# Six weight splits of the recurrence stage, each moved to a later place in VectorE's program

## The reference

```python
z = rmsnorm(h, norm1_g[l])
proj = z @ w_in[l]
q, fl, iv, og, pin, ga, gb = jnp.split(proj, SPLITS, axis=-1)
o_a = hgrn2_mixer(q, fl + b_f[l], iv, og, lb_all[l], head_norm_g[l])   # 8 heads, S_t = diag(f_t) S_{t-1} + (1 - f_t) i_t^T
o_b = pool_mixer(pin, w_pool[l], pool_scale[l])                        # 4 groups: trailing mean minus the frame, a 128 x 128 product each
mix = jax.nn.sigmoid(ga) * (o_a @ w_branch_a[l]) + jax.nn.sigmoid(gb) * (o_b @ w_branch_b[l])
```

## Time and profile before

| | |
|---|---|
| profiled execution | 1472.77 us |
| its span | 1470.9 us |
| median of three runs | 1473.01 us |
| TensorE busy | 1450.9 us (99%) |
| VectorE busy | 834.5 us (57%) |
| ScalarE busy | 691.8 us (47%) |
| granted TensorE clock | 1.000 |

### The profile page before, as it was taken

One profiled execution on the slowest core, in us unless ns is written; L12 is line 12 of the kernel. 1 busy time (PEld: TensorE's weight loads), 2 busy tenths in 40 slices (PEclk: granted clock), 3 DMA queues, 4 the chain that ended last, 5 costly groups with the idle time before them and its releaser, 6 DMA issues.

```text
span 1470.9 us, 26479 instructions
## 1 busy us (share of the span) xinstructions
PE 1450.9 (99%) x11311; PEld 1283.2 (87%) x11311; DVE 834.5 (57%) x1365; ACT 691.8 (47%) x1025; POOL 115.7 (8%) x278
## 2 busy tenths in 40 slices
PE   7999999999999999999999999999999999999998
PEld 7999999999999898998888777788899888778888
DVE  6487977764656566654335787642223566644343
ACT  6565877853443222322233676542222777743232
POOL 0000000000000000000000044300000233320000
PEclk9999999999999999999999999999999999999999
DMA  7222121124322223222334333433223333342222
GB/s 245 87 75 80 60 87 59 59 73 143 131 88 87 86 90 112 87 86 85 103 101 108 63 48 20 77 97 105 86 86 90 67 71 71 72 106 92 86 94 80
DMA packets 138969, 130.25 MB, mean 89 GB/s; under 512 B 26569, under 2 KB 134884, under 8 KB 138596
## 3 DMA queue, kind: packets, MB, share of 16 engines
q1 hardware_dynamic: 134084, 120.39, 26.0%
q0 software_dynamic: 4752, 8.16, 5.3%
q10 hardware_dynamic: 16, 0.00, 0.0%
HBM read 119.69 MB, written 4.26 MB: 84 GB/s over the span
## 4 chain that ended last, share of the span: by engine, by line
PE 91%; DVE 4%; ACT 3%; issue 1%; DMA 0%; SPq 0%; DVEq 0%; ACTq 0%
PE PS L922 79%; PE PS L1248 3%; PE PS L1221 2%; PE PS L1204 2%; DVE wlo L1897 1%; PE PS L1208 1%; PE PS L1207 1%; ACT L1399 1%; PE PS L1033 1%; ACT whi L1399 0%; DMA xt<-in_x 0%; ACT Pm L1399 0%; PE PS L989 0%; PE PS L1089 0%; DVE zlo L1945 0%
## 5 line engine op out<-in xcount | busy, mean ns | idle before, releaser
L922 PE MATMUL PS<-zhi,whi 128*128 128x258 f32 (+2 forms) x1856 | 486.9, 320 | 3.1 <-ACT hT L1399 1.4
L922 PE MATMUL PS<-zhi,wlo 128*128 128x258 f32 (+2 forms) x1856 | 476.8, 314 | 0.0
L922 PE MATMUL PS<-zlo,whi 128*128 128x258 f32 (+2 forms) x1856 | 475.4, 314 | 0.6 <-DVE zlo L1945 0.6
L922 PEld LDWEIGHTS PS<-zhi,whi 128*128 128x128 f32 x1856 | 306.9, 189 | 27.9 <-issue 1.9
L922 PEld LDWEIGHTS PS<-zhi,wlo 128*128 128x128 f32 x1856 | 305.6, 189 | 22.3
L922 PEld LDWEIGHTS PS<-zlo,whi 128*128 128x128 f32 x1856 | 305.5, 189 | 20.8 <-DVE zlo L1945 0.9
L1897 DVE TENSOR_TENSOR wlo<-raw,whi 128x2048 fp32r<-128x2048 f32 (+2 forms) x114 | 247.8, 2174 | 124.7 <-ACT whi L1399 124.6
L1399 ACT ACTIVATE whi<-raw 128x2048 fp32r<-128x2048 f32 (+2 forms) x114 | 207.5, 1820 | 152.7 <-DMA raw<-in_w_up 57.0
L1399 ACT ACTIVATE Pm<-Pm,small 128x144 f32<-128x144 f32 (+3 forms) x128 | 73.1, 572 | 38.5 <-DVE small L2460 38.2
L2460 DVE CUSTOM_DVE_ANT_0 Pm<-PS,cmask 128x144 f32<-128x144 f32 (+3 forms) x128 | 62.9, 504 | 35.8 <-PE PS L1204 21.5
L922 PE MATMUL PS<-glo,whi 128*128 128x512 f32 x176 | 69.9, 397 | 0.0
(11 more groups left out here) (357 smaller groups left out, 2132.9 us busy)
## 6 DMA issues: line engine op xcount, KB each, us to landing
raw<-in_w_in SPq DMA_DIRECT2D x50, 1024.0 KB, 5.3
raw<-in_w_up SPq DMA_DIRECT2D x22, 1024.0 KB, 5.1
raw<-in_w_out SPq DMA_DIRECT2D x8, 1024.0 KB, 5.2
raw<-in_w_down SPq DMA_DIRECT2D x8, 1024.0 KB, 5.1
raw<-in_w_br_mla SPq DMA_DIRECT2D x4, 1024.0 KB, 5.3
raw<-in_w_br_fox SPq DMA_DIRECT2D x4, 1024.0 KB, 5.1
raw<-in_w_down SPq DMA_DIRECT2D x4, 768.0 KB, 4.4
hspill<-hT SPq DMA_DIRECT2D x1, 2112.0 KB, 7.6
```

The source lines that it names most:

```text
L922: ins = mm(o_, l_, r_, start=first, stop=last)
```

## The change

Six entries of the dictionary are moved to a tile that comes later in the order:

```diff
+            for tile, later in ((("og", 1), ("pool", 1)), (("q", 7), ("pool", 3)), (("pin", 3), ("q", 4)),
+                                (("og", 3), ("q", 6)), (("g", 0, 3), ("g", 0, 4)), (("g", 1, 3), ("y", 0, 0))):
+                end_of[later] = end_of.pop(tile)
             waiting = []
             for name, hooks in order:
                 kind, h = name[0:2]
```

## The result

The changed kernel took 1476.79 us in the median of 13 executions (1473.98 to 1478.23), the kernel before 1474.18 us in 13 runs beside it (1472.47 to 1475.03): a ratio of 1.002, 95% interval 1.0012 to 1.0028, so 2.6 us slower. The prediction had said 1474.5 us, +1.5 us, no change that can be told. The time lies outside its range (to 1476.1): the difference is 1.1 us larger than forecast, and the kernel before is 1.2 us slower in 13 runs than in the three that the prediction started from. The kernel before ran 87 more times beside the experiments, and one of these executions, in which the clock was 0.852 and the time 1571.12 us, is left out of the ratios.

A forecast was written before the change was run, and what follows sets the result against it. TensorE, busy 99% of the span, was taken to bound the kernel. Terms 1.94 - 2.02 + 0.53 + 1.01 + 0.03 = +1.49 us on a median of 1473.01 gave 1474.5 us, range 1471.8 to 1476.1.

The forecast's parts named there:

- The two last moves: Splits at g(0, 6) and y(0, 2), put into VectorE's waits of 3.63 and 1.41 us: forecast cost 0.
- the old pause: TensorE's wait for `oblo` before the pool product near 175 us: forecast to go whole, -2.02 us.
- The term for lost clock: At the pauses the change adds: no clock lost, as the clock was 1.00 over the earlier 2.02 us pause.
- line 1023's pause: New TensorE wait near 137 us, behind f4's split before `mul(1)`: forecast +1.94 us, bounds 0 and 2.21.
- f6's two pauses: Around the last pool product: the 0.7 us wait for `pdlo` stays, and a new wait before f6 adds +1.01 us.
- B: Theory set for the experiments: the waits are all, and lost clock is scatter without a place.
- A: Theory set for the experiments: waits cost 1.5 us; clock halved behind new pauses in part of the executions costs the rest.
- Only the pause goes: Rival: slack absorbs VectorE's lag behind q4, new waits shrink, -2.02 us remains: 1471.0 us; chance 0.15.
- The pause stays: Rival: the pool product waits as long for its input or ScalarE; +2.95 us, 1476.0 us; chance 0.07.
- The lag is handed on in full: Rival: ScalarE takes up none of VectorE's lag; +3.9 us, 1476.9 us; chance 0.09.
- The split holds VectorE longer: Rival: twice 2.21 us more where TensorE waits for a product; +5.9 us, 1478.9 us; chance 0.02.
- the estimate of 4.3 us: How long an inserted 2.29 us split would hold VectorE by the skill's drain rule; the prediction's sum did not use it.

The follow-up runs named there:

- all_but_f4: The changed kernel without the move of f4's split, the five other moves kept: 1474.07 us, ratio 0.9997 to the kernel before.
- six_f6_between: All six moves, but f6's split between mul(0) and sub(1) of its pair, not behind pool_prep(3): 1474.79 us, ratio 1.0003 to the kernel before.
- f4_alone: The kernel before with only f4's split moved, from pin3 to q4: 1476.10 us, ratio 1.0014.
- f6_alone: The kernel before with only f6's split moved, from og3 to q6: 1476.33 us, ratio 1.0015.
- f6_between: The kernel before with only q6's split moved behind the pool product and f6's put between mul(0) and sub(1): 1472.14 us, ratio 0.9987.
- f6_high_late: Kernel before with q6's split behind the pool product, f6's between mul(0) and sub(1), ScalarE's high part of f6 at step (1, 9): 1471.09 us, ratio 0.9979.
- after_again: The changed kernel run once more without an edit: 1476.68 us against 1474.31 for the kernel before, ratio 1.0015.

## Why the prediction was wrong

The waits were right. Each place came out to within 0.1 us of the forecast, and the sum too: +1.49 us worked out, 1.52 in the first trace of the changed kernel. The waits in the traces of the other kernels are those of the same working. Their medians are a weaker witness: all_but_f4, six_f6_between and f4_alone agree with the waits alone to within 0.1 us, although their traces show lost clock, but f6_alone is 1.0 us slower than the waits alone give, f6_between 1.0 and f6_high_late 1.2 us faster. The two last moves cost nothing, as said: g(0, 6)'s split leaves 1.42 us of VectorE's 3.63 idle, and behind y(0, 2)'s split VectorE still waits 0.28 us for TensorE, of 1.41 before.

The step that failed is the sentence on the earlier trace rows: the clock was granted in full over the old pause, "so the like pauses that the change adds cost no clock". The term for lost clock was put at nothing from one trace, of a thing that happens in part of the executions. Of the traces with line 1023's pause unfilled, three of five show the clock at half behind it; of those with f6's two pauses, three of four. Where it falls it costs 1.4 to 1.5 us, and 2.7 in one trace. The runs with filled pauses are the test, since the steps stay where they are: 1.9 to 2.1 us come back. (The 0.7 us wait for `pdlo`, which the kernel before has too, is filled with the others; what that part gives alone was not tried.) Of the two theories, B fell: the low clock has its places, and filling the pauses there takes it away. A held in kind, but it missed the time of f4_alone, expected no lost clock in all_but_f4, and priced the filled pauses at half of what came back.

The new pauses are also not quite like the old one. Behind line 1023's pause of 1.8 us stand 68 products of 8 and 16 columns before the stream goes on, and f6's 1.3 us follow 0.7 us with only 6 products between them; behind the old pause the pool product starts at 175.60 and og3's tile at 176.39, without a break. Whether this is why the old pause shows no fall in four traces was not tested.

Waits of 1.5 us and clock of 1.9 to 2.1 us are more than the 2.4 to 2.6 measured. The kernel before would then have to lose some 1 us of its own. Three results fit that: filled, it is 0.75 us faster, though the interval touches no change; f6_between and f6_high_late, which lack its pause of 2.0 us, are 1.0 and 1.2 us better than their waits; and the two filled kernels are 1.24 us apart (1474.59 - 1473.35), near the 1.5 of the waits. Where it loses that stays open: no trace shows it behind the pause, and one of three shows 1.7 us at the program's start, whose cause is open too.

The second error is the base: 1473.01 was the median of three runs, of which two lay at the low end; 13 and 33 runs gave 1474.2 and 1474.3 us. A small slip stands in the chances: the cases named for slower by over 0.2% add up to 0.145 (0.09 + 0.02 + half of 0.07), not 0.13.

Of the rivals none was it. "Only the pause goes" fell with the first wait. "The pause stays" fell too: the pool product starts without a wait. "The lag is handed on in full" named 1476.9 us, and 1476.79 was measured, but that is chance: it named 3.9 us of waiting where 1.5 came, and the lag was taken up just where the earlier trace rows had it. "The split holds VectorE longer" fell as well: the next instruction starts 2.20 us after the split (135.59 to 137.79). The section on the drain that the prediction cites from the Trainium skill ("VectorE: DVE Perf Modes", "The DRAIN you can't avoid") goes on to say that an instruction that is not held starts earlier. So, other than the prediction says, the 2.20 us need not contradict the page; they show that the estimate of 4.3 us does not hold here.

The Trainium skill, "TensorE: Matmul & The Clock Gate", section "A second HAM failure mode: psum-queue depth-cycling", tells of a kernel whose TensorE idles for short times between groups of products so often that its clock falls and rises again and again, and that this costs throughput. The traces of after_again, all_but_f4 and f6_alone agree with it in part: they show 0.50 of the clock behind pauses of 0.7 and 1.3 us, but there the clock falls once and not again and again.

What the change got right is its first entry: turning q6's split and `pool_out` round takes a pause of 2.0 us away. What it got wrong are f4's and f6's new places, each in front of something that TensorE wants at once. With f6's split in VectorE's own gap, and its high part in ScalarE's, the same idea gains 3.2 us.

## What to carry to other kernels

Before an instruction is moved back in an engine's order, look at what stands behind the new place and when the bounding engine wants it; the price is the instruction's start-to-start time less the slack there, and at these places that came out to within 0.1 us. Move such work into a gap in which its engine waits for the bounding engine anyway. And price a pause of TensorE twice: for its length, and for the clock behind it, from several executions and not from one trace; filling the pause with products that nobody reads is a quick test of the second.

## What the runs showed of the hardware

The granted clock fell to half, for 3 to 7 us, behind pauses of 1.3 to 1.9 us, in some executions of a kernel and not in others. In f4_alone it fell while the small products behind the pause still ran, in six_f6_between only 1.7 us after the pause of 1.8 us had ended. The 24 useless products of some 0.12 us each (0.24 from row to row of two) made the kernel 1.9 to 2.1 us faster. A single profiled execution with a mean clock of 1.000 stood for 4 of 24 executions of the changed kernel.
